# The scatter's weighted one-hots on VectorE instead of GpSimd, with all one-hots in 16-bit pairs of tokens

## The chip, the cores and the metric

One core of one Trainium2 chip runs the kernel. The metric is the device time of one execution in microseconds (us). Three runs of the kernel before are given, with their median.

## The reference, cut to what matters

The program is a two-layer decoder trunk for 256 tokens of width 2048. The part that the change touches is the expert retrieval at the end of each layer. For each token and each of 8 heads it picks 16 of 16384 experts. An expert's number is a pair (e1, e2) of numbers below 128. The token's output is a weighted sum of rows of a value table:

```python
eid = e1 * PEER_KEYS + e2                    # PEER_KEYS = 128
g = jax.nn.softmax(cv, axis=-1)
u = jnp.take(u_tab, eid, axis=0)
a = jnp.einsum('td,thkd->thk', xb, u)
coef = g * jax.nn.gelu(a, approximate=False)
vv = jnp.take(v_tab, eid, axis=0)
return jnp.einsum('thk,thkd->td', coef, vv)
```

## The kernel before, in words

The kernel gathers nothing. It multiplies all tokens with the whole of both tables and masks the coefficients in between. Every large product streams its weights through SBUF in slabs of 128x1024 float32 (512 KB), 1312 of them. A ring of 4 slots holds them. SyncE issues the load of a slab (tile w_raw) when TensorE has used the slab four places before it. ScalarE then writes a rounded copy (w_hi, line L505), VectorE writes the remainder (w_lo, L938), and TensorE does 24 matmuls of 256 columns on the slab: 8 blocks times three products (lines L1424, L1425, L1426). Each engine works its list in order, and semaphores join them.

In each of the two layers, `experts(layer)` runs the query product, then the table `u` in 256 slabs, then the table `v` in 256 slabs. From u comes, for each of 128 blocks of experts, a grid of gelu values (tile big, [128 experts, 256 tokens] each). Before v can use a block as coefficients, it has to be multiplied with the weights g, which are zero for all experts that a token has not picked. Making this mask is the *scatter*. For one token, the 128 picks (8 heads of 16) lie on the 128 partitions. A one-hot row of e2 per pick (tile hot2, 128 wide) and a weighted one-hot row of e1 per pick (tile hot1, 64 wide, one half of e1's range at a time) are multiplied by TensorE, which sums over the picks and gives the token's 128x64 grid of weights in PSUM. For precision the weight is split in three bfloat16 parts (WPARTS = 3, tile jw), so a token costs three matmuls of 64 columns.

The scatter is cut in two parts per layer (halves of e1's range). Part 0 runs beside slabs of u, part 1 beside slabs of v. So there are four scatter stages in the program. Each has 8 turns of 8 steps, and a step `s` handles one slab and 4 tokens. Per step the engines do, in their own order:

- VectorE: `lo` of the slab (L938); in part 1 also `c_lo`, the remainder of a coefficient block (L1371); in every second step `spread` (L1320), which multiplies 8 finished tokens of a PSUM bank into the grid; then, after waiting until TensorE has done the scatter step before the last (semaphore s_hot_free, two buffers), `key1` (L1334), the unweighted one-hot of e1, 4 tokens x 64, and `hot2` (L1338), 4 tokens x 128. Both compare the float32 number row `iota` with the float32 picks `jt`, and write bfloat16.
- GpSimd: after waiting for key1, `hot1` (L474): key1 times the three weight parts, 4 tokens x 3 x 64 = 768 elements, all bfloat16.
- TensorE: the slab's 24 matmuls, then, after waiting for hot2 and hot1 of the step and, for a new bank, for the spread that freed it (s_g), the 12 small matmuls of the step (L1777).

GpSimd's other work (sums of squares for the norms, L449, and spilling and reloading the residual, L463 and L483) lies outside these stages.

```python
for s in range(8):                           # VectorE, part 0, in a turn i
    lo(s % 4, i * 8 + (ubase + 8 * SC_FIRST + s))
    scatter(0, i, s)                         # [spread], key1, hot2
```

Of the kernel before, what the change touches and what calls it, by code (L numbers as in the profile page):

```python
# [29 lines left out]
BF16 = mybir.dt.bfloat16  # L30
U32 = mybir.dt.uint32
ALU = mybir.AluOpType
# [75 lines left out]
def decoder_kernel(nc, xT, dense0, dense1, u0, u1, v_tab, keys, gains, gates_in, w_pool, inv_count,  # L108
                   w_glow, w_gate, out):
    ctx = ExitStack()  # L110
    with ctx:
        def sb(name, shape, dt=F32):
            return ctx.enter_context(nc.sbuf_tensor(name, shape, dt))

        def S(name):
            return ctx.enter_context(nc.semaphore(name))
# [11 lines left out]
        gain = sb("gain", [P, 128])  # L128
        gbias = sb("gbias", [P, 2])
        ones = sb("ones", [P, P])  # L130
        iota = sb("iota", [P, P])
        ident = sb("ident", [P, P])
        zrow = sb("zrow", [1, P])
        epst = sb("epst", [P, 1])
# [2 lines left out]
        stdv_base = nc.sbuf_base  # L137
        stdv = sb("stdv", [P, T])

        key1 = nc.alloc_sbuf_tensor_at("key1", [P, 8, HALF], BF16, offset=stdv_base)  # L140
        rstd = sb("rstd", [P, T])
        e12_base = nc.sbuf_base
        e12 = sb("e12", [P, 2, ITEMS, TOPK])
        cv = sb("cv", [P, ITEMS, TOPK])


        hot1 = nc.alloc_sbuf_tensor_at("hot1", [P, 8, WPARTS, HALF], BF16, offset=e12_base)
        hot2 = sb("hot2", [P, 8, P], BF16)
        csum = sb("csum", [P, ITEMS])
        jt = sb("jt", [P, 2, T])  # L150
        jw = sb("jw", [P, WPARTS, T], BF16)
        ps = ctx.enter_context(nc.psum_tensor("ps", [P, 8, 512], F32))


# [26 lines left out]
        s_tk = S("s_tk")  # L181
        s_act = S("s_act")
        s_pool = S("s_pool")
        s_pool_turn = S("s_pool_turn")

        s_gates_ps = S("s_gates_ps")
        s_grow = S("s_grow")
# [89 lines left out]
        def sc_turns(layer, part):  # L277

            return (layer * PARTS + part) * SC_TURNS
# [9 lines left out]
        G_NORM = [0, 16, 32, 48, 64]  # L289
        G_EH, G_PS, G_OH, G_BG = 80, 88, 96, 112  # L290
        N_CONSTS = 5
        POOL_CONSTS = 17
        WG_W = 36


# [54 lines left out]
        def _(pool):  # L350
            count = [0]

            def step(ins):
# [15 lines left out]
            step(pool.memset(ident[:, :], 0.0))  # L369
            step(pool.affine_select(out=ident[:, :], in_=ident[:, :], compare_op=ALU.not_equal, fill=1.0,  # L370
                                    base=0, pattern=[[-1, P]], channel_multiplier=1))
            step(pool.iota(iota[:, :], pattern=[[1, P]], base=0, channel_multiplier=0,
                           allow_small_or_imprecise_dtypes=True))

            step(pool.memset(tri01[:, :], 1.0))
# [78 lines left out]
            for layer in range(2):  # L454
                if layer == 1:
                    exponents()
                add_squares(2 * layer + 1, KB)


                pool.wait_ge(s_evac, BLOCK0["wq", layer])  # L460
                for c in range(PIECES):
                    pool.wait_ge(s_used, SLAB0["wq", layer] + 3 * c + 1)
                    pool.dma_start(spill[:, PIECE * c:PIECE * (c + 1)], at(XT + PIECE * c, PIECE)).then_inc(s_spill, 16)  # L463

                for part in range(PARTS):
                    with pool.Fori(0, SC_TURNS) as i:
                        for q in range(8):


                            pool.wait_ge(s_key1, i * 8 + (sc_turns(layer, part) * 8 + q + 1))  # L470
                            pool.sem_inc(s_pool_turn, 1)
                            b = 4 * (q % 2)
                            w = jw[:, :, bass.ds(i * SC_TOKENS + 4 * q, 4)].rearrange("p c t -> p t c")
                            pool.tensor_tensor(hot1[:, b:b + 4, :, :],  # L474
                                               key1[:, b:b + 4, :].unsqueeze(2).broadcast_to([P, 4, WPARTS, HALF]),
                                               w.unsqueeze(3).broadcast_to([P, 4, WPARTS, HALF]),
                                               ALU.mult).then_inc(s_hot1, 1)


                pool.wait_ge(s_spill, 16 * PIECES * (layer + 1))  # L480
                for c in range(PIECES):
                    pool.wait_ge(s_used, SLAB0["vt", layer] + HALF + KB + 4 * c)
                    pool.dma_start(at(XT + PIECE * c, PIECE), spill[:, PIECE * c:PIECE * (c + 1)]).then_inc(s_reload, 16)  # L483
                add_squares(2 * layer + 2, KB // 2)
                if layer == 0:
                    pool.wait_ge(s_used, SLAB0["qk", 1])
                    pool.dma_start(at(K_KEYS, 2048), keys[1]).then_inc(s_keys, 16)
                    pool.dma_start(big[0:G_RANK, O_WGATE:O_WGATE + 1024], w_gate).then_inc(s_consts, 16)
                    pool.dma_start(at(O_WGL, 256), w_glow).then_inc(s_consts, 16)
# [437 lines left out]
        def _(dve):  # L927
# [343 lines left out]
            def experts(layer):  # L1271
# [34 lines left out]
                dve.wait_ge(s_jt_ps, layer + 1)  # L1306
                dve.tensor_copy(jt[:, :, :].rearrange("p c t -> p (c t)"), bank(3))
                chain(dve.tensor_copy(rstd[:, :], bank(4, T)))
                for c in range(WPARTS):
                    chain(dve.tensor_copy(jw[:, c, :], rstd[:, :]))  # L1310
                    if c < WPARTS - 1:
                        chain(dve.tensor_tensor(rstd[:, :], rstd[:, :], jw[:, c, :], ALU.subtract))

                def spread(part, i, k):

# [6 lines left out]
                def scatter(part, i, s, first=False):  # L1322


                    done = sc_turns(layer, part)
                    if s in (4, 6):
                        spread(part, i, (s - 4) // 2)
                    elif s in (0, 2) and not first:
                        spread(part, i - 1, s // 2 + 2)

                    dve.wait_ge(s_hot_free, i * 8 + (done * 8 + s + 1))
                    t0, b = i * SC_TOKENS + 4 * s, 4 * (s % 2)
                    num = jt[:, :, t0:t0 + 4] if isinstance(i, int) else jt[:, :, bass.ds(t0, 4)]
                    dve.tensor_tensor(key1[:, b:b + 4, :],  # L1334
                                      iota[:, HALF * part:HALF * (part + 1)].unsqueeze(1).broadcast_to([P, 4, HALF]),
                                      num[:, 0, :].unsqueeze(2).broadcast_to([P, 4, HALF]),
                                      ALU.is_equal).then_inc(s_key1, 1)
                    dve.tensor_tensor(hot2[:, b:b + 4, :], iota[:, :].unsqueeze(1).broadcast_to([P, 4, P]),  # L1338
                                      num[:, 1, :].unsqueeze(2).broadcast_to([P, 4, P]),
                                      ALU.is_equal).then_inc(s_hot2, 1)  # L1340

                def scatter_rest(part):
                    for k in (2, 3):
# [78 lines left out]
        def _(pe):  # L1422
# [298 lines left out]
            def experts(layer):  # L1721
# [43 lines left out]
                def scatter(part, i, s):  # L1765


                    done = sc_turns(layer, part)
                    if s % 2 == 0:

                        pe.wait_ge(s_g, i * 4 + (done * 4 + s // 2 + 1))
                    pe.wait_ge(s_hot2, i * 8 + (done * 8 + s + 1))
                    pe.wait_ge(s_hot1, i * 8 + (done * 8 + s + 1))
                    for x in range(4):
                        t = 4 * (s % 2) + x
                        for c in range(WPARTS):
                            ins = pe.matmul(ps[:, 4 + s // 2, HALF * t:HALF * (t + 1)], hot2[:, t, :],  # L1777
                                            hot1[:, t, c, :], start=c == 0, stop=c == WPARTS - 1)
                    ins.then_inc(s_hot_free, 1)

                with pe.Fori(0, SC_FIRST - 1) as i:
# [120 lines left out]
```

## Time and profile before

| | |
|---|---|
| median of 3 runs | 4343.08 us (4334.75, 4343.08, 4348.55) |
| span of the profiled execution | 4344.9 us |
| its own time, otherwise than by its span | not given apart |
| PE busy | 4117.4 us, 95% of the span |
| DVE (VectorE) busy | 2832.0 us, 65% |
| ACT (ScalarE) busy | 1848.2 us, 43% |
| POOL (GpSimd) busy | 701.0 us, 16% |
| HBM traffic | 162 GB/s over the span |

The profiled span stands 1.8 us above the median of the runs and inside their range. In the tables of the profile, PE is TensorE's matmuls and PEld its weight loads, which overlap them. The mean durations of matmuls are longer than their distance, because they are pipelined, and starts tell more. "Idle before" is the time in which the engine had nothing to do before an instruction, with what ended it.

### The profile page before, as it was taken

What the parts mean: (1) busy time and instruction counts of PE and PEld (TensorE: products, weight loads), DVE (VectorE), ACT (ScalarE), POOL (GpSimd) and SP (SyncE); (2) the same over time, 40 slices, a digit from 0 to 9 for tenths busy, and PEclk for the clock granted to TensorE, in tenths of its full rate; (3) what the DMA queues carried; (4) which work ended last, traced back from release to release, by engine and by line L of the source; (5) the groups of instructions that cost most, each with busy time, mean ns of one, the idle gap of its engine ahead of it and who ended that gap; (6) DMA issues with size and microseconds to landing.
All of it is one profiled execution on the core that took longest, in us unless ns stands there. A gap on an engine that the chain in (4) does not pass through costs nothing.

```text
span 4344.9 us, 90772 instructions
## 1 busy us (share of the span) xinstructions
PE 4117.4 (95%) x34860; PEld 4038.3 (93%) x34860; DVE 2832.0 (65%) x3745; ACT 1848.2 (43%) x2326; POOL 701.0 (16%) x397
## 2 busy tenths in 40 slices
PE   8999999989998899999999999999989988899998
PEld 7999999988998899999898899999989988899998
DVE  4554778789559965444545555878897489755444
ACT  4444444433443344444444444444434533344443
POOL 1211000054114510000002010000353045300000
PEclk9999999999999999999999999999999999999999
DMA  5455566644553356555554456666544533465554
GB/s 177 144 162 173 174 183 181 180 131 134 171 160 121 125 172 194 181 182 183 160 150 129 145 167 181 182 181 183 150 131 145 182 127 121 135 201 183 183 182 152
DMA packets 193647, 705.65 MB, mean 162 GB/s; under 512 B 21808, under 2 KB 22000, under 8 KB 193184
## 3 DMA queue, kind: packets, MB, share of 16 engines
q1 hardware_dynamic: 190224, 692.21, 51.8%
q0 software_dynamic: 3344, 12.32, 0.7%
q8 instruction: 57, 0.93, 0.1%
q14 instruction: 22, 0.18, 0.0%
HBM read 698.16 MB, written 6.29 MB: 162 GB/s over the span
## 4 chain that ended last, share of the span: by engine, by line
PE 78%; DVE 9%; POOL 5%; issue 4%; DMA 3%; ACT 1%; DVEq 0%; SPq 0%; POOLq 0%; ACTq 0%
PE ps L1424 24%; PE ps L1425 24%; PE ps L1426 24%; POOL hot L474 4%; DVE w_lo L938 4%; DMA w_raw<-in_v_tab 2%; PE ps L1777 1%; DMA w_raw<-in_dense 1%; DVE key L1334 1%; DVE hot L1338 1%; DVE big L1320 1%; DVE big L998 1%; ACT w_hi L505 1%; PE ps L1687 0%; PE ps L1686 0%
## 5 line engine op out<-in xcount | busy, mean ns | idle before, releaser
L1424 PE MATMUL ps<-act_lo_t,w_hi 128*128 128x256 f32 x10112 | 2924.6, 289 | 67.3 <-DVE act_lo_t L987 36.8
L1425 PE MATMUL ps<-act_hi_t,w_lo 128*128 128x256 f32 x10112 | 2890.4, 286 | 0.0
L1426 PE MATMUL ps<-act_hi_t,w_hi 128*128 128x256 f32 x10112 | 2888.5, 286 | 0.0
L938 DVE TENSOR_TENSOR w_lo<-w_raw,w_hi 128x1024 fp32r<-128x1024 f32 x1312 | 1834.9, 1400 | 1368.9 <-ACT w_hi L505 1358.3
L505 ACT ACTIVATE w_hi<-w_raw 128x1024 fp32r<-128x1024 f32 x1312 | 1388.4, 1059 | 1845.9 <-DMA w_raw<-in_v_tab 1004.1
L1424 PEld LDWEIGHTS ps<-act_lo_t,w_hi 128*128 128x128 f32 x10112 | 1969.7, 195 | 83.4 <-issue 50.6
L1425 PEld LDWEIGHTS ps<-act_hi_t,w_lo 128*128 128x128 f32 x10112 | 1971.5, 195 | 0.1
L1426 PEld LDWEIGHTS ps<-act_hi_t,w_hi 128*128 128x128 f32 x10112 | 1970.0, 195 | 0.0
L474 POOL TENSOR_TENSOR hot<-key,jw 128x768 bf16<-128x768 bf16 x256 | 557.0, 2181 | 1672.5 <-DVE key L1334 1672.5
L1777 PE MATMUL ps<-hot,hot 128*128 128x64 bf16 x3072 | 137.8, 196 | 115.4 <-POOL hot L474 114.9
L858 ACT ACTIVATE big<-ps 128x256 f32 (+1 forms) x256 | 98.6, 385 | 320.6 <-PE ps L1426 320.2
L1777 PEld LDWEIGHTS ps<-hot,hot 128*128 128x128 bf16 x3072 | 108.3, 100 | 134.0 <-issue 87.9
L1338 DVE TENSOR_TENSOR hot<-iota,jt 128x512 bf16<-128x512 f32 x256 | 174.6, 682 | 0.0
L449 POOL TENSOR_TENSOR rstd<-big 128x256 f32<-128x256 f32 x4 | 4.4, 1105 | 1047.7 <-ACT big L587 844.7
L1320 DVE TENSOR_TENSOR big<-big,ps 128x512 f32 (+1 forms) x128 | 167.3, 1308 | 8.4 <-PE ps L1777 8.4
L1334 DVE TENSOR_TENSOR key<-iota,jt 128x256 bf16<-128x256 f32 x256 | 122.4, 478 | 73.3 <-PE ps L1777 73.3
L1371 DVE TENSOR_TENSOR act_lo_t<-big,act_hi_t 128x256 fp32r<-128x256 f32 x384 | 162.2, 423 | 0.0
L893 ACT ACTIVATE act_hi_t<-big 128x256 fp32r (+1 forms) x384 | 153.2, 400 | 0.0
L858 ACT ACT_TABLE_LOAD x34 | 43.6, 1283 | 93.2 <-PE ps L1426 93.2
L449 POOL TENSOR_TENSOR rstd<-rstd,big 128x256 f32<-128x256 f32 x40 | 48.6, 1214 | 114.9 <-ACT big L611 114.0
L563 ACT ACTIVATE big<-ps 128x256 f32<-128x256 f32 (+1 forms) x56 | 21.4, 382 | 97.1 <-PE ps L1426 96.9
L1685 PE MATMUL ps<-w_hi,act_lo_t 128*128 128x512 f32 x128 | 51.3, 401 | 0.0
(218 smaller groups left out, 1345.6 us busy)
## 6 DMA issues: line engine op xcount, KB each, us to landing
w_raw<-in_u SPq DMA_DIRECT2D x512, 512.0 KB, 3.5
w_raw<-in_v_tab SPq DMA_DIRECT2D x512, 512.0 KB, 3.7
w_raw<-in_dense SPq DMA_DIRECT2D x288, 512.0 KB, 3.6
x_spill<-big POOLq DMA_DIRECT2D x16, 256.0 KB, 4.8
big<-x_spill POOLq DMA_DIRECT2D x16, 256.0 KB, 4.4
big<-in_xT SPq DMA_DIRECT2D x4, 512.0 KB, 5.3
big<-in_keys POOLq DMA_DIRECT2D x2, 1024.0 KB, 10.4
out<-big SPq DMA_DIRECT2D x4, 512.0 KB, 2.7
```

What stands on the lines that cost most here:

```text
L474: pool.tensor_tensor(hot1[:, b:b + 4, :, :], key1[:, b:b + 4, :].unsqueeze(2).broadcast_to([P, 4, WPARTS, HALF]), w.unsqueeze(3).broadcast ...
L505: act.activation(w_hi[:, slot, :], w_raw[:, slot, :], ACT.Copy).then_inc(s_hi, 1)
L893: act.activation(act_hi_t[:, buf, :], src, ACT.Copy).then_inc(s_chi, 1)
L938: dve.tensor_tensor(w_lo[:, slot, :], w_raw[:, slot, :], w_hi[:, slot, :].bitcast(F32), ALU.subtract).then_inc(s_lo, 1)
L1320: dve.tensor_tensor(dst, dst, bank(4 + k, 512, 8), ALU.mult).then_inc(s_g, 1)
L1334: dve.tensor_tensor(key1[:, b:b + 4, :], iota[:, HALF * part:HALF * (part + 1)].unsqueeze(1).broadcast_to([P, 4, HALF]), num[:, 0, :].unsq ...
L1338: dve.tensor_tensor(hot2[:, b:b + 4, :], iota[:, :].unsqueeze(1).broadcast_to([P, 4, P]), num[:, 1, :].unsqueeze(2).broadcast_to([P, 4, P] ...
L1371: dve.tensor_tensor(act_lo_t[:, buf, :], src, act_hi_t[:, buf, :].bitcast(F32), ALU.subtract).then_inc(s_clo, 1)
L1424: pe.matmul(out, wh, xl, start=start, stop=False, **kw)
L1425: pe.matmul(out, wl, xh, start=False, stop=False, **kw)
L1426: return pe.matmul(out, wh, xh, start=False, stop=stop, **kw)
L1777: ins = pe.matmul(ps[:, 4 + s // 2, HALF * t:HALF * (t + 1)], hot2[:, t, :], hot1[:, t, c, :], start=c == 0, stop=c == WPARTS - 1)
```

## The change

The product that makes hot1 moves from GpSimd's list to VectorE's, right behind hot2 of the same step, with a wait for key1. GpSimd's loop over it is gone, and so is a semaphore that only it used. All operands of the three one-hot operations become bfloat16 (`jt`, and a second number row `iota2`; the old `iota` shrinks to the 16 numbers that another place uses). Every one-hot tile is laid out so that two tokens lie side by side in memory: `hot2` is [4 pairs, 128, 2], `key1` [4 pairs, 64, 2], `hot1` [4 pairs, 3, 64, 2], and `jw` [128 pairs, 3, 2]. TensorE therefore reads one token's weights and columns with a step of two elements. Numbers of instructions on TensorE, ScalarE and SyncE, and their order, stay the same.

```diff
-        iota = sb("iota", [P, P])
+        iota = sb("iota", [P, TOPK])
+        iota2 = sb("iota2", [P, P, 2], BF16)
...
-        key1 = nc.alloc_sbuf_tensor_at("key1", [P, 8, HALF], BF16, offset=stdv_base)
+        key1 = nc.alloc_sbuf_tensor_at("key1", [P, 4, HALF, 2], BF16, offset=stdv_base)
...
-        hot1 = nc.alloc_sbuf_tensor_at("hot1", [P, 8, WPARTS, HALF], BF16, offset=e12_base)
-        hot2 = sb("hot2", [P, 8, P], BF16)
+        hot1 = nc.alloc_sbuf_tensor_at("hot1", [P, 4, WPARTS, HALF, 2], BF16, offset=e12_base)
+        hot2 = sb("hot2", [P, 4, P, 2], BF16)
         csum = sb("csum", [P, ITEMS])
-        jt = sb("jt", [P, 2, T])
-        jw = sb("jw", [P, WPARTS, T], BF16)
+        jt = sb("jt", [P, 2, T], BF16)
+        jw = sb("jw", [P, T // 2, WPARTS, 2], BF16)
...
-                for part in range(PARTS):
-                    with pool.Fori(0, SC_TURNS) as i:
-                        for q in range(8):
-                            pool.wait_ge(s_key1, i * 8 + (sc_turns(layer, part) * 8 + q + 1))
-                            pool.sem_inc(s_pool_turn, 1)
-                            b = 4 * (q % 2)
-                            w = jw[:, :, bass.ds(i * SC_TOKENS + 4 * q, 4)].rearrange("p c t -> p t c")
-                            pool.tensor_tensor(hot1[:, b:b + 4, :, :],
-                                               key1[:, b:b + 4, :].unsqueeze(2).broadcast_to([P, 4, WPARTS, HALF]),
-                                               w.unsqueeze(3).broadcast_to([P, 4, WPARTS, HALF]),
-                                               ALU.mult).then_inc(s_hot1, 1)
...
                     dve.wait_ge(s_hot_free, i * 8 + (done * 8 + s + 1))
-                    t0, b = i * SC_TOKENS + 4 * s, 4 * (s % 2)
+                    t0, b = i * SC_TOKENS + 4 * s, 2 * (s % 2)
                     num = jt[:, :, t0:t0 + 4] if isinstance(i, int) else jt[:, :, bass.ds(t0, 4)]
-                    dve.tensor_tensor(key1[:, b:b + 4, :],
-                                      iota[:, HALF * part:HALF * (part + 1)].unsqueeze(1).broadcast_to([P, 4, HALF]),
-                                      num[:, 0, :].unsqueeze(2).broadcast_to([P, 4, HALF]),
+                    num = num.rearrange("p c (a x) -> p c a x", x=2)
+                    p0 = i * (SC_TOKENS // 2) + 2 * s
+                    w = jw[:, p0:p0 + 2, :, :] if isinstance(i, int) else jw[:, bass.ds(p0, 2), :, :]
+                    dve.tensor_tensor(key1[:, b:b + 2, :, :],
+                                      iota2[:, HALF * part:HALF * (part + 1), :].unsqueeze(1).broadcast_to([P, 2, HALF, 2]),
+                                      num[:, 0, :, :].unsqueeze(2).broadcast_to([P, 2, HALF, 2]),
                                       ALU.is_equal).then_inc(s_key1, 1)
-                    dve.tensor_tensor(hot2[:, b:b + 4, :], iota[:, :].unsqueeze(1).broadcast_to([P, 4, P]),
-                                      num[:, 1, :].unsqueeze(2).broadcast_to([P, 4, P]),
+                    dve.tensor_tensor(hot2[:, b:b + 2, :, :], iota2[:, :, :].unsqueeze(1).broadcast_to([P, 2, P, 2]),
+                                      num[:, 1, :, :].unsqueeze(2).broadcast_to([P, 2, P, 2]),
                                       ALU.is_equal).then_inc(s_hot2, 1)
+
+                    dve.wait_ge(s_key1, i * 8 + (done * 8 + s + 1))
+                    dve.tensor_tensor(hot1[:, b:b + 2, :, :, :],
+                                      key1[:, b:b + 2, :, :].unsqueeze(2).broadcast_to([P, 2, WPARTS, HALF, 2]),
+                                      w.unsqueeze(3).broadcast_to([P, 2, WPARTS, HALF, 2]),
+                                      ALU.mult).then_inc(s_hot1, 1)
...
-                            ins = pe.matmul(ps[:, 4 + s // 2, HALF * t:HALF * (t + 1)], hot2[:, t, :],
-                                            hot1[:, t, c, :], start=c == 0, stop=c == WPARTS - 1)
+                            ins = pe.matmul(ps[:, 4 + s // 2, HALF * t:HALF * (t + 1)], hot2[:, t // 2, :, t % 2],
+                                            hot1[:, t // 2, c, :, t % 2], start=c == 0, stop=c == WPARTS - 1)
```

Left out above: the number row iota2 is written once at the start by GpSimd, and the three copies that fill jw write the new order.

VectorE, one step of the loop of part 1 (c_lo, key1, hot2, and the lo of the next step), before; ISA and REGISTER_ALU rows set addresses and take waits:

```order
L1371 ISA [waits s_chi]
L1371 TENSOR_TENSOR act_lo_t<-big,act_hi_t 128x256
L1331 REGISTER_ALU
L1334 ISA [waits s_hot_free]
L1334 TENSOR_TENSOR key_50<-iota,jt 128x256
L1338 ISA
L1338 TENSOR_TENSOR hot<-iota,jt 128x512
L937 REGISTER_ALU
L938 TENSOR_TENSOR w_lo<-w_raw,w_hi 128x1024 [waits s_hi]
```

The same step with the change:

```order
L1369 ISA [waits s_chi]
L1369 TENSOR_TENSOR act_lo_t<-big,act_hi_t 128x256
L1320 REGISTER_ALU
L1326 ISA [waits s_hot_free]
L1326 TENSOR_TENSOR key_50<-iota,jt 128x256
L1330 ISA
L1330 TENSOR_TENSOR hot<-iota,jt 128x512
L1335 ISA [waits s_key1]
L1335 TENSOR_TENSOR hot_51<-key_50,jw 128x768
L925 REGISTER_ALU
L926 TENSOR_TENSOR w_lo<-w_raw,w_hi 128x1024 [waits s_hi]
```

One instruction of 768 elements with a wait on s_key1 has come in between hot2 and the next lo.

GpSimd, the start of the loop that goes away, before (the eight pairs of it follow the last spill DMA):

```order
L463 DMA x_spill<-big 128x512 [waits s_used] x7
L466 UNCONDITIONAL_BRANCH
L466 ISA
L474 ISA [waits s_key1]
L474 TENSOR_TENSOR hot_51<-key_50,jw 128x768
L470 REGISTER_ALU
```

With the change none of the L474 rows is left, and the wait for the spill's end follows the spill's DMAs directly.

## Rows read from the trace of the kernel before

**Rows 1.** The page: busy time, and busy tenths in 40 slices
```profile
span 4344.9 us, 90772 instructions
PE 4117.4 (95%) x34860; PEld 4038.3 (93%) x34860; DVE 2832.0 (65%) x3745; ACT 1848.2 (43%) x2326; POOL 701.0 (16%) x397
...
PE   8999999989998899999999999999989988899998
...
POOL 1211000054114510000002010000353045300000
```

**Rows 2.** Windows: the four scatter stages, first to last burst; busy us (x instructions), clock, DMA
```profile
core 0: us, PE busy (x) PEld busy (x) DVE busy (x) ACT busy (x) POOL busy (x), PEclk, DMA share, GB/s
859.70:1107.50 247.80, 222.35 (x2271) 217.18 (x2270) 223.19 (x219) 96.09 (x110) 133.41 (x63) 0.95 0.44 134
1280.00:1544.50 264.50, 225.68 (x2269) 219.35 (x2268) 243.12 (x275) 86.05 (x126) 140.41 (x62) 0.94 0.38 125
3073.20:3326.00 252.80, 226.11 (x2271) 220.72 (x2270) 224.52 (x219) 95.82 (x110) 130.55 (x63) 0.93 0.44 131
3498.60:3765.20 266.60, 227.38 (x2270) 221.74 (x2270) 242.39 (x275) 84.67 (x124) 141.94 (x62) 0.93 0.39 124
```

**Rows 3.** Windows: a stretch of the u table without scatter
```profile
600.00:850.00 250.00, 249.74 (x2082) 249.56 (x2082) 194.37 (x432) 112.80 (x134) 0.00 (x0) 1.00 0.61 181
```

**Rows 4.** TensorE's timeline, the scatter's bursts of one piece of stage four: start, us
```profile
3676.83 0.52 PE L1777 MATMUL ps<-hot,hot 128*128 128x64 bf16 x12
3684.28 0.80 PE L1777 MATMUL ps<-hot,hot 128*128 128x64 bf16 x12 [3.97 <-POOL hot L474]
...
3693.54 0.52 PE L1777 MATMUL ps<-hot,hot 128*128 128x64 bf16 x12
3696.85 0.52 PE L1777 MATMUL ps<-hot,hot 128*128 128x64 bf16 x12
```

**Rows 5.** Waits, longest in total: who waited for whom, us, times, longest
```profile
PE ps L1777 <- POOL hot L474: 114.9, 46, 4.3
```

**Rows 6.** GpSimd's timeline over the same piece
```profile
3678.55 7.04 POOL L474 TENSOR_TENSOR hot<-key,jw 128x768 bf16<-128x768 bf16 x2 [3.23 <-DVE key L1334]
3686.13 1.70 POOL L474 TENSOR_TENSOR hot<-key,jw 128x768 bf16<-128x768 bf16 x1 [0.54 <-DVE key L1334]
```

**Rows 7.** VectorE's timeline over the same piece
```profile
3676.66 1.31 DVE L1320 TENSOR_TENSOR big<-big,ps 128x512 f32 x1
3677.87 0.42 DVE L1334 TENSOR_TENSOR key<-iota,jt 128x256 bf16<-128x256 f32 x1
3678.20 0.69 DVE L1338 TENSOR_TENSOR hot<-iota,jt 128x512 bf16<-128x512 f32 x1
3678.81 1.22 DVE L938 TENSOR_TENSOR w_lo<-w_raw,w_hi 128x1024 fp32r<-128x1024 f32 x1
3679.94 0.42 DVE L1371 TENSOR_TENSOR act_lo_t<-big,act_hi_t 128x256 fp32r<-128x256 f32 x1
3680.28 0.42 DVE L1334 TENSOR_TENSOR key<-iota,jt 128x256 bf16<-128x256 f32 x1
...
3685.22 0.65 DVE L1334 TENSOR_TENSOR key<-iota,jt 128x256 bf16<-128x256 f32 x1 [1.29 <-PE ps L1777]
3685.79 0.68 DVE L1338 TENSOR_TENSOR hot<-iota,jt 128x512 bf16<-128x512 f32 x1
3686.40 2.51 DVE L938 TENSOR_TENSOR w_lo<-w_raw,w_hi 128x1024 fp32r<-128x1024 f32 x1
```

**Rows 8.** Groups by shape on VectorE: in stage one, and in the stretch without scatter
```profile
L938 DVE TENSOR_TENSOR w_lo<-w_raw,w_hi 128x1024 fp32r<-128x1024 f32 x64 | 129.3, 2021 | 10.9 <-ACT w_hi L505 10.9
L938 DVE TENSOR_TENSOR w_lo<-w_raw,w_hi 128x1024 fp32r<-128x1024 f32 x87 | 106.5, 1225 | 48.3 <-ACT w_hi L505 45.6
```

**Rows 9.** Groups by shape: a copy that VectorE does faster than a two-input operation
```profile
L1234 DVE COPY big<-big 128x256 f32 x30 | 8.6, 286 | 0.0
```

**Rows 10.** Groups by shape: weight loads of the scatter and of a slab
```profile
L1777 PEld LDWEIGHTS ps<-hot,hot 128*128 128x128 bf16 x3072 | 108.3, 100 | 134.0 <-issue 87.9 <-DVE big L1320 36.9
L1424 PEld LDWEIGHTS ps<-act_lo_t,w_hi 128*128 128x128 f32 x10112 | 1969.7, 195 | 83.4 <-issue 50.6 <-DVE w_lo L938 25.0 <-DVE act_lo_t L987 5.5
```

More of the change, by code:

```diff
@@ L183, in decoder_kernel @@
         s_pool = S("s_pool")
-        s_pool_turn = S("s_pool_turn")
         s_gates_ps = S("s_gates_ps")
@@ L291, in decoder_kernel @@
         N_CONSTS = 5
-        POOL_CONSTS = 17
+        POOL_CONSTS = 18
         WG_W = 36
@@ L371, in _ @@
                                     base=0, pattern=[[-1, P]], channel_multiplier=1))
-            step(pool.iota(iota[:, :], pattern=[[1, P]], base=0, channel_multiplier=0,
+            step(pool.iota(iota[:, :], pattern=[[1, TOPK]], base=0, channel_multiplier=0,
+                           allow_small_or_imprecise_dtypes=True))
+            step(pool.iota(iota2[:, :, :], pattern=[[1, P], [0, 2]], base=0, channel_multiplier=0,
                            allow_small_or_imprecise_dtypes=True))
@@ L1308, in experts @@
                 chain(dve.tensor_copy(rstd[:, :], bank(4, T)))
+                pairs = rstd[:, :].rearrange("p (t x) -> p t x", x=2)
                 for c in range(WPARTS):
-                    chain(dve.tensor_copy(jw[:, c, :], rstd[:, :]))
+                    chain(dve.tensor_copy(jw[:, :, c, :], pairs))
                     if c < WPARTS - 1:
-                        chain(dve.tensor_tensor(rstd[:, :], rstd[:, :], jw[:, c, :], ALU.subtract))
+                        chain(dve.tensor_tensor(pairs, pairs, jw[:, :, c, :], ALU.subtract))
                 def spread(part, i, k):
```

## The prediction
> **What bounds the kernel now.** I read the page first. TensorE is busy for 95% of the span and GpSimd for 16%, with its work in two short humps of the 40 slices, and TensorE's row has its 8s there too [rows 1]. So the question is what TensorE loses beside GpSimd. The windows from the first to the last burst of small matmuls of each scatter stage answer that: 247.8, 264.5, 252.8 and 266.6 us, 1031.7 together [rows 2]. Each holds 64 bursts, so 63 distances, 252 in all, of 4.094 us on average.
>
> What would it be without loss? A stretch of the u table without scatter has 2082 matmuls in 250.0 us, 0.120 us each, so 2.88 us for a slab of 24 [rows 3]. In the timeline of TensorE the undisturbed distance from burst to burst is 3.31 us (3693.54 to 3696.85) [rows 4]. The 12 small matmuls therefore cost 0.43 us, 0.036 each. I counted all 252 distances in that timeline: 143 are under 3.4 us, 46 lie between 3.4 and 4.5, and 63 are longer, as the one of 7.45 us (3676.83 to 3684.28) [rows 4]. At 3.31 us throughout, the stages would take 252 x 3.31 = 834.1 us. The loss is 197.6 us, and it is the most that the change can give back if TensorE's own work stays the same.
>
> Who causes it? The table of waits names GpSimd's product for 114.9 us of TensorE's idle time in 46 waits [rows 5]. The rest is lower clock: the four stages show 0.93 to 0.95 of the full clock, the stretch without scatter 1.00 [rows 2, 3]. After a stall of 4 us TensorE runs part of the next slabs at 1.2 instead of 2.4 GHz.
>
> Why is the product late? GpSimd needs 1.70 us for it, but two that follow each other took 7.04 us [rows 6]. In that time VectorE worked without a pause [rows 7]. The other way round, when the product runs, VectorE's lo takes 2.51 us instead of 1.22 [rows 7]. In stage one its mean is 2.02 us, in the stretch without scatter 1.23 [rows 8]. So each engine holds the other up, and a product that starts behind VectorE's back-to-back work is not done until VectorE has to wait for TensorE. The middle class of distances comes from it as well: 2.44 (lo, start to next start) + 0.34 + 0.33 + 0.61 + half of 1.21 makes 4.3 us for VectorE's step in part 1, and 4.0 without c_lo.
>
> **The change part by part.** *GpSimd.* It loses its 256 products, and with them the lock-out in both directions: lo falls from about 2.0 to 1.22 us in these stages. What stands behind the loop in its queue, the reload of the residual, waits for slabs of v that TensorE uses after the scatter, so nothing there comes earlier or later. At the start it writes one number row more, beside work that nobody waits for yet: 0.
>
> *VectorE.* Its row starts give the price of an instruction as the distance to the next start: lo 1.13, c_lo 0.34, spread 1.21 (once in two steps, so 0.61 a step), key1 0.33, hot2 0.61 [rows 7]. The durations 0.42, 0.68 and 1.22 us for 256, 512 and 1024 elements are 0.15 us plus 1.04 ns an element, and the next one starts some 0.08 us before the end. The product of 768 elements with only 16-bit operands has no row on VectorE. Upper bound: the same slope, 0.15 + 0.80 - 0.08 = 0.87 us. Lower bound: two elements at a time, 0.15 + 0.40 - 0.08 = 0.47 us. That VectorE can do two at a time is seen in a copy of 256 elements that takes 0.286 us, against 0.42 for two inputs [rows 9]; 0.15 + 0.13 is 0.28. By the same two rates key1 costs 0.33 or 0.20, and hot2 0.61 or 0.34.
>
> A step of VectorE is then:
> - at two elements: 1.13 + 0.61 + 0.20 + 0.34 + 0.47 = 2.75 us in part 0, and 3.09 with c_lo in part 1;
> - at one element: 1.13 + 0.61 + 0.33 + 0.61 + 0.87 = 3.55 us in part 0, and 3.89 in part 1.
>
> I take two elements. All three operands are 16-bit now, with two neighbouring tokens in each 4-byte word, so the product moves 384 words, and in words it is nearest to the rows between 256 and 512. Then VectorE stays under TensorE's 3.31 us in both parts, with 0.22 us to spare in part 1, and TensorE is the bound.
>
> On this rate the Trainium skill has a rule. "VectorE: DVE Perf Modes", section "The perf-mode tier table", gives a two-input operation twice the rate if everything is 16-bit in SBUF; the page "Vector Engine (DVE) Microarchitecture Reference", section 5.1, adds that an operand whose single element is read again and again stays at the single rate. The pairs avoid that case. By this rule the sum is the forecast, without it the single-rate rival; no row of this trace shows it.
>
> *The new wait for key1.* It stands behind hot2 and before everything that VectorE does next. key1 is done about 0.29 us after its start, and hot2 runs until 0.6 us or later after it. So hot2 covers it. Without that cover it would cost 0.1 us a step, which part 1's 0.22 us still hold.
>
> *Lateness.* hot1 of a step can start once the burst two steps before is over, and TensorE needs it 2 x 3.31 - 0.43 = 6.2 us later. VectorE has 1.0 us of one-hots and at most 2.1 us of other work in that time, so a late semaphore does not reach TensorE.
>
> *TensorE.* The same instructions, but weights and columns are read with a step of two 16-bit elements. I take 0: columns at 4-byte distance are what each float32 matmul of a slab reads at 0.120 us for 256. The weight side is a rival below.
>
> *What is late next.* At 3.31 us a slab, loads and ScalarE must deliver faster than at 4.09, but the stretch without scatter shows them at 2.88 us a slab and 181 GB/s [rows 3]. They hold.
>
> **The sum.** -197.6 us for the 252 distances, and +10 us for what I expect to remain: the filling of the first turn of each stage, and single late slabs. That gives -188 us. The profiled span is 4344.9 us, so the new one is 4157; it stands 1.8 us above the median of 4343.1, so the median becomes 4155. The lower end is the whole loss and a run as far below the median as the lowest shown, 8 us: 4343 - 198 - 8 = 4137, say 4138.
>
> **The rivals.**
> *Single rate (8%).* The change does not get the double rate it is laid out for. VectorE is the bound at 3.55 and 3.89 us: 126 x 3.55 + 126 x 3.89 = 937 us, 94 less than now, time 4249. For it: hot2 now writes 16-bit elements and still takes 0.68 us, as 512 float32 would. Against it: its inputs are float32.
> *Only the product is double (6%).* The compares stay at 0.33 and 0.61. Part 0 takes 3.15 us and stays under TensorE, part 1 takes 3.49: 126 x 3.31 + 126 x 3.49 = 857 us, with the 10 us time 4178.
> *The weight loads get somewhat slower (12%).* A load of the scatter's 128 columns of 16 bits has records of 100 ns, one of a slab 195 [rows 10]. It is fast now, and the step of two may cost part of this. A pair of load and matmul of 0.058 us instead of 0.036 makes 3.57 us a step, 900 us in all, with the 10 us time 4221. Smaller ones lie between.
> *The weight loads lose all their speed (5%), the slower side.* If a pair takes what a slab's pair takes, 0.120 us, the burst is 1.44 us and the step 4.32: 252 x 4.32 = 1089 us, 57 more than now, time 4400. It decides from 0.101 us a pair on, where the step is the present 4.094 us. For it: the new layout has only one wanted weight in every 4-byte word. Against it: nothing in the rows shows a strided load, and the matmul of 0.036 us leaves little room, so either a load keeps up or everything shows.
> The Trainium skill speaks on this rival both ways: "TensorE: Matmul & The Clock Gate", section "Weight-path perf modes", says that the fast load reads 32 bits at a time, two bf16 weights, which a step of two spoils, and also that packed or strided columns are allowed. By the first the burst grows, by the second it doesn't.
> *Nothing gained (3%).* GpSimd's product was late for a reason that stays, and VectorE is late in its place: within 0.3%, 4343.
>
> **How the numbers follow.** The forecast has 66%, at 4138 to 4175. The range goes up to 4225: it takes in the second and nearly all of the third rival, and leaves out the single rate, the full slowdown, no gain, and a little of the rest, under 2 in 10. A measurement of this kernel can tell about 0.3%, 13 us, from no change. Faster by more than this are all cases but two: 92%. The same 3%, slower 5%.
>
> **What would show it.** In the profile after: no product on GpSimd; lo at 1.22 us throughout; the product on VectorE near 0.55 us, key1 near 0.29, hot2 near 0.42; bursts 3.31 us apart; a clock of 1.00 in the four stages; stages of 209 us. If key1 and hot2 keep 0.42 and 0.68, the compares are at the single rate. If the bursts last longer than 0.43 us beyond the slab's 2.88, the weight loads are slower. I am wrong altogether if TensorE still stands for microseconds before its small matmuls.

## The result, and the profile after

The changed kernel takes 4148.72 us (median of 4 runs, 4146.02 to 4150.45), the kernel before in all its runs by then 4338.91 (4334.03 to 4348.55). The ratio of the two is 0.9561, with a 95% interval of 0.9546 to 0.9575. The forecast was 4155, range 4138 to 4225. The profiled execution took 4150.45 us, its span is 4148.7.

The page after: first busy times, then two rows of the 40 slices.

```profile
span 4148.7 us, 90161 instructions
PE 4056.4 (98%) x34860; PEld 3989.7 (96%) x34860; DVE 2624.9 (63%) x4001; ACT 1848.2 (45%) x2326; POOL 146.1 (4%) x142
...
PE   8999999999999999999899999999999999999998
...
POOL 1111000000000000000003020000000000000000
```

GpSimd's two humps are gone, and TensorE's 8s at their places with them [rows 1]. VectorE has 256 instructions more and yet 207 us less busy time (2832.0 to 2624.9). The windows of the four scatter stages after, first to last burst (PE, PEld, DVE, ACT, POOL busy us with instructions, clock, DMA share, GB/s):

```profile
859.93:1069.51 209.58, 209.58 (x2270) 206.87 (x2269) 175.62 (x280) 95.79 (x110) 0.00 (x0) 1.00 0.52 158
1239.73:1449.55 209.82, 209.82 (x2270) 207.11 (x2269) 193.52 (x337) 84.72 (x124) 0.00 (x0) 1.00 0.49 158
2980.68:3190.26 209.58, 209.58 (x2271) 206.87 (x2269) 175.80 (x280) 95.88 (x110) 0.00 (x0) 1.00 0.53 159
3359.25:3569.12 209.87, 209.87 (x2269) 207.16 (x2269) 193.26 (x337) 84.73 (x124) 0.00 (x0) 1.00 0.49 158
sum 838.85, PE 838.85 PEld 828.01 DVE 738.21 ACT 361.13 POOL 0.00; mean PE 209.71 PEld 207.00 DVE 184.55 ACT 90.28 POOL 0.00
```

TensorE is busy for the whole of each window at a clock of 1.00, where it was 0.93 to 0.95 [rows 2]. The stages take 838.85 us instead of 1031.7, which is 192.8 of the 196.2 us between the two spans. The other 3.4 us lie in the stretches outside them, which sum to 3313.2 us before and 3309.85 after; the two stretches that follow a part 0 became 2.3 and 3.6 us shorter, and the one between the layers 2.4 longer. Inside the stages TensorE's busy time fell from 901.5 to 838.85 us and its idle time from 130.2 to 0.

TensorE's timeline of a piece of stage four (start, us), and the groups of the product, key1 and hot2 (busy us and mean ns, then idle us before them with what ended it):

```profile
3422.75 0.54 PE L1775 MATMUL ps<-hot,hot 128*128 128x64 bf16 x12
3426.08 0.54 PE L1775 MATMUL ps<-hot,hot 128*128 128x64 bf16 x12
3429.40 0.54 PE L1775 MATMUL ps<-hot,hot 128*128 128x64 bf16 x12
```

```profile
L1335 DVE TENSOR_TENSOR hot<-key,jw 128x768 bf16<-128x768 bf16 x256 | 141.7, 553 | 0.0
...
L1326 DVE TENSOR_TENSOR key<-iota,jt 128x256 bf16<-128x256 bf16 x256 | 73.8, 288 | 58.1 <-PE ps L1775 57.8
L1330 DVE TENSOR_TENSOR hot<-iota,jt 128x512 bf16<-128x512 bf16 x256 | 107.5, 420 | 0.0
```

The bursts are 3.327 us apart, and 250 of the 252 distances are under 3.4 us; before, 143 were, as the prediction counted. The three one-hot operations take 0.553, 0.288 and 0.420 us. VectorE waits for TensorE before key1 (57.8 us in all), and the small matmuls no longer wait for one of its one-hots.

### The profile page after: what moved, and what is told of

Its sections match the earlier page's. It is cut to its first block, busy times and chain, and to the rows that moved or that the text cites. A ratio compares the mean times of both kernels' runs of the same rounds, so it can differ in the third digit from the quotient of the medians.

```text
span 4148.7 us, 90161 instructions
## 1 busy us (share of the span) xinstructions
PE 4056.4 (98%) x34860; PEld 3989.7 (96%) x34860; DVE 2624.9 (63%) x4001; ACT 1848.2 (45%) x2326; POOL 146.1 (4%) x142
## 4 chain that ended last, share of the span: by engine, by line
PE 92%; DVE 4%; DMA 2%; ACT 1%; issue 1%; POOL 0%; SPq 0%; DVEq 0%; POOLq 0%; ACTq 0%
PE ps L1422 29%; PE ps L1423 28%; PE ps L1424 28%; PE ps L1775 2%; DMA w_raw<-in_dense 1%; DVE w_lo L926 1%; DVE big L986 1%; DMA w_raw<-in_v_tab 1%; ACT w_hi L493 1%; PE ps L1683 0%; PE ps L1684 0%; PE ps L1685 0%; PE ps L1629 0%; DVE act_lo_t L975 0%; PE ps L1731 0%
## 5 line engine op out<-in xcount | busy, mean ns | idle before, releaser
L926 DVE TENSOR_TENSOR w_lo<-w_raw,w_hi 128x1024 fp32r<-128x1024 f32 x1312 | 1619.4, 1235 | 1392.6 <-ACT w_hi L493 1379.2
L1422 PEld LDWEIGHTS ps<-act_lo_t,w_hi 128*128 128x128 f32 x10112 | 1948.4, 193 | 57.5 <-issue 40.3
L1423 PEld LDWEIGHTS ps<-act_hi_t,w_lo 128*128 128x128 f32 x10112 | 1950.7, 193 | 0.1
L1424 PEld LDWEIGHTS ps<-act_hi_t,w_hi 128*128 128x128 f32 x10112 | 1949.1, 193 | 0.0
L1335 DVE TENSOR_TENSOR hot<-key,jw 128x768 bf16<-128x768 bf16 x256 | 141.7, 553 | 0.0
L1326 DVE TENSOR_TENSOR key<-iota,jt 128x256 bf16<-128x256 bf16 x256 | 73.8, 288 | 58.1 <-PE ps L1775 57.8
L1330 DVE TENSOR_TENSOR hot<-iota,jt 128x512 bf16<-128x512 bf16 x256 | 107.5, 420 | 0.0
```

The source lines that it names most:

```text
L926: dve.tensor_tensor(w_lo[:, slot, :], w_raw[:, slot, :], w_hi[:, slot, :].bitcast(F32), ALU.subtract).then_inc(s_lo, 1)
L1330: dve.tensor_tensor(hot2[:, b:b + 2, :, :], iota2[:, :, :].unsqueeze(1).broadcast_to([P, 2, P, 2]), num[:, 1, :, :].unsqueeze(2).broadcast ...
L1335: dve.tensor_tensor(hot1[:, b:b + 2, :, :, :], key1[:, b:b + 2, :, :].unsqueeze(2).broadcast_to([P, 2, WPARTS, HALF, 2]), w.unsqueeze(3).b ...
L1422: pe.matmul(out, wh, xl, start=start, stop=False, **kw)
L1423: pe.matmul(out, wl, xh, start=False, stop=False, **kw)
L1424: return pe.matmul(out, wh, xh, start=False, stop=stop, **kw)
```

## The experiments

Theory A is the prediction's: a product on GpSimd and VectorE's operations hold each other up, and TensorE is the bound as soon as VectorE's step is shorter than its own. Its rivals: B, the shorter compares are what pays; C, it is the hand-off from VectorE to GpSimd to TensorE that costs, whatever VectorE does meanwhile. "Stages" below is the sum of the four windows from first to last burst: 1031.7 us before and 838.85 after. Of this, part 0 has 500.6 and 419.2, part 1 531.1 and 419.7.

### Layout without the move: e1_layout_only

```diff
-                    dve.wait_ge(s_key1, ...)
-                    dve.tensor_tensor(hot1[:, b:b + 2, ...], ..., ALU.mult).then_inc(s_hot1, 1)
...
+                            pool.wait_ge(s_key1, ...)
+                            pool.tensor_tensor(hot1[:, b:b + 2, ...], ..., ALU.mult).then_inc(s_hot1, 1)
```

> One part of the change undone: the product goes back to GpSimd, the 16-bit pairs stay. Theory A (both engines hold each other up at SBUF): lo still takes 2.5 us beside a product, VectorE's step is 2.44 + 0.61 + 0.20 + 0.34 = 3.6 us in part 0 and 3.9 in part 1 where they meet, and a product that starts behind VectorE's back-to-back work is still late; some 0.4 us a step are saved by the shorter compares, at most 100 us of the 193: time 4240 to 4300. Theory B (the double rate of the compares is what pays): 4150 to 4170. Theory C (the hand-off to GpSimd and back is what costs, whatever VectorE does): no change, 4335 to 4345.

Measured: 4219.93 us, ratio to before 0.9716 (0.9699 to 0.9732). It falls below A's interval and far above B's. The windows:

```profile
860.17:1069.75 209.58, 209.58 (x2271) 206.87 (x2269) 180.54 (x218) 95.86 (x110) 141.96 (x63) 1.00 0.52 158
1240.77:1485.71 244.94, 223.71 (x2270) 219.64 (x2269) 219.96 (x275) 84.71 (x124) 163.41 (x62) 0.94 0.41 135
```

Part 0 is as fast as in the changed kernel, with the product still on GpSimd. Theory C is out: in part 0 the hand-off is there in every step, and TensorE never waits. The two stages of part 1 are 35 and 32 us longer than the changed kernel's. What I had missed is that not every product holds an operation up: in this trace 43 operations of VectorE are lengthened by more than 0.9 us in the two stages of part 0, and 86 in those of part 1. The section on e10_spread_behind, below, follows single products.

### Move without the layout: e2_move_only

```diff
+                    dve.wait_ge(s_key1, i * 8 + (done * 8 + s + 1))
+                    w = jw[:, :, t0:t0 + 4] if isinstance(i, int) else jw[:, :, bass.ds(t0, 4)]
+                    dve.tensor_tensor(hot1[:, b:b + 4, :, :],
+                                      key1[:, b:b + 4, :].unsqueeze(2).broadcast_to([P, 4, WPARTS, HALF]),
+                                      w.rearrange("p c t -> p t c").unsqueeze(3).broadcast_to([P, 4, WPARTS, HALF]),
+                                      ALU.mult).then_inc(s_hot1, 1)
```

(to the kernel before, without GpSimd's loop)

> The other part alone: the product moves to VectorE, layout and types stay as before (float32 compares, one token after the other). Theory A with the single rate: key1 0.42, hot2 0.68, product 0.95 us; VectorE is the bound at 3.55 and 3.89 us a step, stages of 224 and 245 us, time 4149 + 98 = 4247. If the product of 16-bit operands gets the double rate without the pairs: product 0.55 us, steps of 3.3 and 3.49 us, time 4170. Theory B (the layout pays): about 4340.

Measured: 4234.73 us, ratio 0.9756 (0.974 to 0.9772). Its groups and one window of each part:

```profile
L1329 DVE TENSOR_TENSOR hot<-key,jw 128x768 bf16<-128x768 bf16 x256 | 244.7, 956 | 0.0
...
L1323 DVE TENSOR_TENSOR hot<-iota,jt 128x512 bf16<-128x512 f32 x256 | 176.4, 689 | 0.0
```

```profile
861.50:1082.35 220.85, 213.53 (x2271) 207.73 (x2269) 220.85 (x281) 95.69 (x110) 0.00 (x0) 1.00 0.49 150
1252.98:1493.89 240.91, 214.91 (x2271) 208.18 (x2269) 238.90 (x337) 85.17 (x125) 0.00 (x0) 1.00 0.43 137
```

The product takes 0.956 us at the single rate. VectorE is busy throughout part 0 and for 238.90 of 240.91 us in part 1: it is the bound, at 220.85 / 63 = 3.51 and 3.82 us a step, where the single-rate rival of the prediction had 3.55 and 3.89. TensorE's pauses (busy 213.53 of 220.85 us) are short here, and its clock stays at 1.00 in both windows.

### 16-bit types without pairs: e3_move_16bit_no_pairs

Edit: as e2_move_only, with jt and a number row in bfloat16.

> The product on VectorE and all operands 16-bit, but tokens one after the other, so that the pick or weight is one element read again and again. If the double rate needs pairs in every operand: key1 0.42, hot2 0.68, product 0.95 us, as in e2_move_only, time 4235. If 16-bit types are enough: 0.29, 0.42 and 0.55 us, time 4145 to 4149. The single rate of the product in e2_move_only alone does not tell this for the compares, whose inputs were float32 there.

Measured: 4234.49 us, ratio 0.9758 (0.9728 to 0.9789).

```profile
L1332 DVE TENSOR_TENSOR hot<-key,jw 128x768 bf16<-128x768 bf16 x256 | 242.2, 946 | 0.0
...
L1326 DVE TENSOR_TENSOR hot<-iotab,jt 128x512 bf16<-128x512 bf16 x256 | 173.9, 679 | 0.0
```

All operands are 16-bit, and none of the three is faster than in e2_move_only. So it takes the pairs as well to get the double rate. That is the case that the Trainium skill ("Vector Engine (DVE) Microarchitecture Reference", section 5.1) describes for one element read again and again, and this run agrees with it: 0.946 against 0.553 us.

### Compares at the single rate: e4_f32_compares

```diff
-        iota2 = sb("iota2", [P, P, 2], BF16)
+        iota2 = sb("iota2", [P, P, 2])
-        jt = sb("jt", [P, 2, T], BF16)
+        jt = sb("jt", [P, 2, T])
```

> The changed kernel with the compares' inputs in float32 again (number row and picks), pairs and everything else as changed: key1 0.42, hot2 0.68, product 0.55 us. By row distances VectorE's step is 3.15 us in part 0, which hides under TensorE's 3.33, and 3.49 in part 1, which doesn't: 126 x (3.49 - 3.33) = 20 us more than the changed kernel, time 4169, all of it in the two stages of part 1. If VectorE has no work to spare even in part 0: 4190 or more. If VectorE's work is hidden anyway: 4149.

Measured: 4169.19 us, ratio 0.9602 (0.9586 to 0.9618).

```profile
860.30:1069.88 209.58, 209.58 (x2270) 206.87 (x2269) 199.88 (x280) 96.13 (x110) 0.00 (x0) 1.00 0.53 158
1239.95:1457.46 217.51, 213.80 (x2269) 208.46 (x2269) 214.37 (x337) 84.75 (x124) 0.00 (x0) 1.00 0.47 152
```

Part 0 hides 24 us more of VectorE's work (199.88 against 175.62) at no cost, and part 1 does not: 217.51 us, 3.45 a step. This is the mixed rival of the prediction (3.15 and 3.49). So a VectorE step of 3.15 us, summed from starts, is hidden and one of 3.45 us, as measured, is not; TensorE's own 3.33 lies between.

### GpSimd's product beside the changed kernel: e6_pool_beside

```diff
+        spare = sb("spare", [P, 2, WPARTS, HALF, 2], BF16)
...
+                            pool.wait_ge(s_key1, ...)
+                            pool.tensor_tensor(spare[...], iota2[:, 0:HALF, :]..., iota2[:, 0:6, :]..., ALU.mult)
```

> The changed kernel, and beside it GpSimd makes a product of the same size and types at the same places (after each key1) from a constant into a spare tile that nobody reads. The output is the same. Theory A: lo takes 2.5 us where they meet, VectorE's step becomes up to 2.44 + 0.61 + 1.01 = 4.06 us in part 0 and 4.40 in part 1, and VectorE becomes the bound: up to 1066 us for the stages against 839, time 4250 to 4376, without anybody waiting for GpSimd. Theory C (only the product's place in the chain cost time): lo stays at 1.22 us, time 4149.

Measured: 4300.21 us, ratio 0.9905 (0.9888 to 0.9921), inside theory A's interval. A product that nobody waits for costs 151 us against the changed kernel. The places differ from what A said: lo has a mean of 1.282 us over the whole kernel (1.235 after), and the operation that pays most is VectorE's own product, since it stands right behind hot2:

```profile
L1348 DVE TENSOR_TENSOR hot<-key,jw x256: 537/1818/1857, 854.3 to 3709.6; 128x768 bf16<-128x768 bf16 x128
```

(shortest, median and longest in ns.) The median is 1.82 instead of 0.54 us, 1.28 more, which is what lo had paid before (2.51 against 1.22) [rows 7].

### When does a shut-out product get in? e10_spread_behind

The timelines of e1_layout_only answer what e1 had left open. A piece of part 1, VectorE first, then GpSimd:

```profile
1338.42 1.22 DVE L939 TENSOR_TENSOR w_lo<-w_raw,w_hi 128x1024 fp32r<-128x1024 f32 x1
1339.55 0.43 DVE L1376 TENSOR_TENSOR act_lo_t<-big,act_hi_t 128x256 fp32r<-128x256 f32 x1
1339.89 0.29 DVE L1339 TENSOR_TENSOR key<-iota,jt 128x256 bf16<-128x256 bf16 x1
1340.09 0.42 DVE L1343 TENSOR_TENSOR hot<-iota,jt 128x512 bf16<-128x512 bf16 x1
1340.43 1.23 DVE L939 TENSOR_TENSOR w_lo<-w_raw,w_hi 128x1024 fp32r<-128x1024 f32 x1
1341.56 0.42 DVE L1376 TENSOR_TENSOR act_lo_t<-big,act_hi_t 128x256 fp32r<-128x256 f32 x1
1341.90 1.27 DVE L1322 TENSOR_TENSOR big<-big,ps 128x512 f32 x1
```

```profile
1338.44 6.31 POOL L475 TENSOR_TENSOR hot<-key,jw 128x768 bf16<-128x768 bf16 x2 [1.99 <-DVE key L1339]
```

```profile
1343.46 0.52 PE L1782 MATMUL ps<-hot,hot 128*128 128x64 bf16 x12 [1.91 <-POOL hot L475]
```

The product is offered at 1338.44, just after a lo has started. TensorE gets it at 1343.46. It cannot have run before about 1341.9, for the shortest such product of this trace takes 1.46 us. At 1341.90 VectorE starts spread, its one operation that reads PSUM and has one SBUF input. The trace of before has the same:

```profile
L474 POOL TENSOR_TENSOR hot<-key,jw x256: 1488/1703/5587, 856.1 to 3759.9; 128x768 bf16<-128x768 bf16 x128
```

There 37 products last over 3.5 us, and 34 of them end 1.43 to 1.48 us after a spread's start (the expectation below says "all but one", which was a misread figure: it is all but three). The other three ran behind a hot2 after which VectorE stood idle for 0.9 to 1.3 us, so idle time lets a product in as well. All 37 belong to the 128 steps that have a place for spread ahead of key1 (even s), and none to the other 128 steps, though 91 products there were offered at the same point, 0.26 us after key1's end. And spread never pays: its 128 instructions before lie between 1.225 and 1.379 us.

So I moved spread and nothing else, in the kernel before:

```diff
-                    if s in (4, 6):
-                        spread(part, i, (s - 4) // 2)
-                    elif s in (0, 2) and not first:
-                        spread(part, i - 1, s // 2 + 2)
                     dve.wait_ge(s_hot_free, ...)
...
                     dve.tensor_tensor(hot2[:, b:b + 4, :], ...)
+                    if s in (4, 6):
+                        spread(part, i, (s - 4) // 2)
+                    elif s in (0, 2) and not first:
+                        spread(part, i - 1, s // 2 + 2)
```

> The kernel before, with one thing moved: VectorE's spread (its one operation that reads PSUM and has one SBUF input) stands behind hot2 of the same step instead of ahead of key1. Nothing is added or made faster. Theory A1 (a product of GpSimd that has been shut out gets in when spread runs; in the trace of before 37 products longer than 3.5 us end 1.43 to 1.47 us after a spread's start, all but one): behind a product that starts at hot2 of such a step nothing shuts it out any more, and another one waits at most 2.4 us instead of 3.9. Fewer and shorter stalls of TensorE before its small matmuls, time 4220 to 4300, products of over 5 us gone. Theory A2 (it gets in only when VectorE is idle, which happens after spread by chance): no change, 4335 to 4345, or worse.

Measured: 4200.68 us, ratio 0.9681 (0.9665 to 0.9697), 19 us below the interval of theory A1. All 256 products:

```profile
L474 POOL TENSOR_TENSOR hot<-key,jw x256: 1671/1701/1712, 856.0 to 3615.4; 128x768 bf16<-128x768 bf16 x128
```

Before, the longest was 5.587 us; now none is shut out. The steps whose products had been shut out have spread behind hot2 now. The move does a second thing, which no run separates from this: in these steps key1 and hot2 no longer stand behind spread's 1.21 us. VectorE's timeline shows what remains:

```profile
3422.17 0.68 DVE L1333 TENSOR_TENSOR hot<-iota,jt 128x512 bf16<-128x512 f32 x1
3422.78 2.51 DVE L938 TENSOR_TENSOR w_lo<-w_raw,w_hi 128x1024 fp32r<-128x1024 f32 x1
...
3425.88 0.68 DVE L1333 TENSOR_TENSOR hot<-iota,jt 128x512 bf16<-128x512 f32 x1
3426.48 1.34 DVE L1320 TENSOR_TENSOR big<-big,ps 128x512 f32 x1
3427.74 1.26 DVE L938 TENSOR_TENSOR w_lo<-w_raw,w_hi 128x1024 fp32r<-128x1024 f32 x1
```

Behind hot2 stands a lo in one step and pays 1.29 us, and spread in the next and pays nothing. VectorE's step is then 1.13 + 0.34 + 0.33 + 0.61 + 0.61 + 1.29 / 2 = 3.67 us in part 1; the stages give 229.7 / 63 = 3.65. The place of one instruction alone brings 139 us (4340.02 to 4200.68), where the whole change brings 190.

### Layout, and spread behind: e11_layout_spread_behind

Edit: e1_layout_only with the edit of e10_spread_behind.

> e1_layout_only (16-bit pairs, product on GpSimd) with spread moved behind hot2 as in e10_spread_behind, where every second product ran beside spread at no cost and every other one held lo up by 1.29 us. Then VectorE's step is 1.13 + 0.34 + 0.61 + 0.20 + 0.34 + 1.29 / 2 = 3.27 us in part 1 and 2.93 in part 0, both under TensorE's 3.33: the stages fall to 838 us and the time to 4149 to 4152, that of the changed kernel, without moving the product. If lo is held up in every step with these shorter one-hots: 3.91 us in part 1, time 4220.

Measured: 4152.29 us, ratio 0.9558 (0.954 to 0.9576). The changed kernel's ratio is 0.9561 (0.9546 to 0.9575), so no difference between the two can be told, with the product on GpSimd here. All 252 distances are under 3.4 us, and the stages sum to 838.3 us. This time shows that VectorE's step stays under TensorE's 3.33 us, and it doesn't measure the 1.29 / 2 = 0.65 us. The trace does: lo and c_lo are longer by 0.6 us a step together in part 1, near it, and lo by 0.26 us in part 0.

### How TensorE reads: e5_packed_weights, e5_packed_both

```diff
-  hot2[:, t // 2, :, t % 2]
+  hot2[:, t // 2, HALF * (t % 2):HALF * (t % 2 + 1), :]
-  hot1[:, t // 2, c, :, t % 2]
+  hot1[:, t // 2, c, 32 * (t % 2):32 * (t % 2) + 32, :]
```

(the second pair in e5_packed_both only; both read other elements than the scatter needs, so that only their times count)

> The changed kernel, but the weight loads read 128 neighbouring elements instead of every second one, so that the scatter's grids are wrong. If the strided weight loads cost the 0.013 us a step: bursts 3.314 us apart as before. If the strided columns do: 3.327 stays.

> As e5_packed_weights, and the moving columns are read packed too, the grids wrong as well. If both accesses share the cost, the distance falls in two steps; 3.314 us here in any case, and if it stays 3.327 the cause is not how TensorE reads.

Measured: distance of bursts 3.327 us with packed weights, 3.320 with both packed, in one run each (4148.36 and 4140.95 us in all). No cost of the step of two is seen for the weight loads. For the columns it costs 0.007 us a step, 1.8 us in all; the 7 us between the two times are no more than runs of one kernel differ. The rest of the 0.013 us against the 3.314 of before and of e2_move_only stays: e3_move_16bit_no_pairs, packed too, has 3.320 as its median distance in part 0, where e2_move_only has 3.314. What makes these 0.006 us is open; they are worth 1.5 us.

### Both packed and paired: e9_doubled_scalars, after_again

```diff
+        jt = sb("jt", [P, 2, T, 2], BF16)
+        jw = sb("jw", [P, T, WPARTS, 2], BF16)
...
+                    dve.tensor_tensor(hot2[:, b:b + 4, :].rearrange("p a (n x) -> p a n x", x=2),
+                                      full.unsqueeze(1).broadcast_to([P, 4, P // 2, 2]),
+                                      num[:, 1, :, :].unsqueeze(2).broadcast_to([P, 4, P // 2, 2]),
+                                      ALU.is_equal).then_inc(s_hot2, 1)
```

> A version that may beat both: tokens one after the other again, so that TensorE reads packed weights and columns, and instead of the tokens the picks and weight parts are stored twice (jt and jw with a last dimension of 2 equal values), so that VectorE still reads 16-bit pairs. If VectorE keeps the double rate (product 0.55, key1 0.29, hot2 0.42 us) and the 0.013 us a step of the changed kernel are TensorE's step of two: 3.314 us a step, 252 x 0.013 = 3.3 us less, time 4145. If the pairs must be two tokens for the double rate: as with the move alone, 4235. If the 0.013 us has another cause: 4149.

> The changed kernel once more, on the same chip as the three beside it: 4149, bursts 3.327 us apart.

Measured, as medians of five runs each: 4151.67 us (ratio 0.9556, 0.9543 to 0.9569) against 4146.69 for the changed kernel (0.9545, 0.9532 to 0.9558). VectorE keeps the double rate (0.553, 0.288 and 0.420 us), so the pair may as well be one value stored twice. The expected 3.314 us a step did not come: the distance is 3.320 us, and the stages sum to 836.6 us against 838.6. Those 2.0 us are visible in the trace and not in the times. No version here beats the changed kernel by anything that the runs can tell.

## Why the prediction was right, point by point

**The bound and the sum.** The 252 distances carried the loss: 197.6 us were to be had, 192.8 came. Of the missing 4.8, the step is 3.327 instead of 3.314 us (3.3 us), and 1.5 are that the floor was taken as 3.31 and that two single distances are longer. The 10 us kept back for first turns and late slabs were too much; 0.5 us of that remained. The forecast of 4155 stood 6 us high: 4.8 because it counted on 188 us where 192.8 came, and 3.4 for the stretches outside the stages, which it left as they were, less 1.8 because the span no longer stands above the median. "The rest is lower clock" was loose: 114.9 us of the loss were waits for the product and 62.7 slower running, and the remaining 15 waits of a slab's first matmul for c_lo (9.8) and lo (4.8). Neither touches the sum, which went by distances.

**VectorE's prices.** 0.15 us plus half of 1.04 ns an element gave 0.55, 0.28 and 0.42 us; measured are 0.553, 0.288 and 0.420. No row of before spoke for the double rate of a two-input operation, and e3_move_16bit_no_pairs shows that it hangs on the pairs which the prediction named. The row distances gave steps of 3.15 and 3.49 us for compares at the single rate, and e4_f32_compares shows part 0 hidden and 3.45 in part 1. For the single rate they gave 3.55 and 3.89; measured 3.51 and 3.82. The sum of starts was 1 to 2% high each time. In the paragraph on lateness, "at most 2.1 us of other work" counts half a spread; a step that has one does 2.7, still far from the 6.2 us there.

**The wait for key1.** The product has no idle time before it (0.0 in its row), so hot2 covers the wait.

**TensorE.** I took 0 for the step of two and kept 17% for slower weight loads. Weight loads cost nothing, columns 0.007 us a step. The Trainium skill ("TensorE: Matmul & The Clock Gate", section "Weight-path perf modes") says that the fast weight load reads 32 bits at a time and that its columns may be packed or strided. That a step of two spoils it was my inference, not the page's, and the trace speaks against it: 3.327 us a step with packed and with strided weights.

**The clock.** It returned to 1.00 once the stalls were gone, as the row of the plain stretch said.

**Where the prediction's mechanism was incomplete.** The step was: "a product that starts behind VectorE's back-to-back work is not done until VectorE has to wait for TensorE." In its place the runs show that it is done beside the next spread, without VectorE being idle (34 of the 37 long products before), and that no product of a step without spread is shut out so long (0 of 128). I had taken the wait for TensorE, which follows spread in these rows, for the cause. The forecast did not need the difference, since it took the product away altogether. The expectation of e1_layout_only did, and missed by 20 us: it let products and two-input operations meet in every step. It also hid from me that the order alone was worth 139 us. So the time came out by the right bound and the right prices, and this step was not put to the test by it.

**What the change consists of.** By themselves the move brings 107 us (4342.25 to 4234.73) and the layout 122 (to 4219.93), in part 0 the layout all of it. Together they bring 190 (4338.91 to 4148.72), less than the sum: each makes room on VectorE, and once its step is below TensorE's 3.33 us no more room is needed.

## What to carry to other kernels

Where GpSimd works beside VectorE, add up the time not only of each engine but of what runs side by side. In this kernel a GpSimd product was paid by the operation with two SBUF inputs that VectorE started next to it, and cost nothing beside the one that reads PSUM, so that one belongs behind the release. Whether this holds for other shapes and operations was not run. Before moving work from one engine to another, try the order of what is already there. And count the limit of the step first: once VectorE's step was below TensorE's, three different versions took the same time within what the runs can tell (4148.72, 4151.67 and 4152.29 us).

## What the runs showed of the hardware that was not expected

- A GpSimd product of 768 16-bit elements (1.47 us alone) lengthens the operation with two SBUF inputs that VectorE starts after the product has got in, by up to 1.3 us, whichever it is: lo 1.22 to 2.51, the 16-bit product 0.54 to 1.82 in e6_pool_beside, key1 0.28 to 1.54 and c_lo 0.42 to 1.69 in e1_layout_only. hot2, which runs when the product is offered, is not lengthened (at most 0.73 us before). Spread, with one input in PSUM, is never lengthened.
- The other way round, a GpSimd operation can be shut out by a dense row of such operations: its records grow to 5.6 us before and to 6.5 in e6_pool_beside, where 48 of the 50 over 3.5 us end 1.40 to 1.44 us after a spread's start. All products over 3.5 us (37 before, 16 in e1_layout_only, 50 in e6_pool_beside) belong to steps with spread ahead of key1.
- Why a product is shut out in some of these steps and not in others was not found: before, 37 of 128 were, and all 128 were offered 0.26 to 0.28 us after key1's end.
- The two-input operations here reach twice the rate when every operand's innermost pair lies in neighbouring 16-bit elements, even if both are the same value (0.553 us for 768 elements in the changed kernel and in e9_doubled_scalars); with a single repeated 16-bit element they don't (0.946 in e3_move_16bit_no_pairs).
